# Attention probabilities with keys on the partitions, after a separate pass for the maxima, in a two-layer hybrid decoder trunk

## What is computed

```
# fox, one head of width 64
s = (q @ k.T) * 64**-0.5
s = s + cum[:, None] - cum_k[None, :]        # cumulated log forget gates
s = where(key <= query, s, -1e30)
out = softmax(s) @ v
# dsa, one head: the same without cum, and only over each query's topk = 64 keys
score = sum_j relu(iq_j @ ik.T / 8) * iw_j   # 16 indexer heads choose the keys
```

## Time and profile before

| | |
|---|---|
| median of 3 runs | 2811.59 us |
| the profiled execution | 2811.41 us, of which the span of the trace is 2809.6 us |
| busy share of the span | PE 95%, PE's weight loads 91%, DVE 63%, ACT 49%, POOL 0% |
| chain that ended last | PE 89%, DVE 6%, ACT 3%, issue 2%, DMA 1% |
| TensorE clock granted, mean over the span | 0.938 of full |
| layer 0, first indexer score to first product of the output projection | 333.26 to 504.68 us |

### The profile page before, as it was taken

How to read it: one execution, slowest core, us unless ns; L and a number is a source line. 1 busy time by engine, 2 the same in 40 slices (tenths; PEclk the granted TensorE clock), 3 DMA queues, 4 the chain that set the end, 5 groups by cost and what they waited for, 6 DMA issues and landing times.

```text
span 2809.6 us, 56056 instructions
## 1 busy us (share of the span) xinstructions
PE 2668.1 (95%) x21786; PEld 2548.4 (91%) x21786; DVE 1782.2 (63%) x2890; ACT 1366.1 (49%) x2051; POOL 11.9 (0%) x19
## 2 busy tenths in 40 slices
PE   5989999989999999999979899999899999999997
PEld 5989866989999999999979898669899999999997
DVE  6777555576666666544487775655766666665445
ACT  5444443456555555433364444444566665653333
POOL 0000000000000000000000000000000000000000
PEclk8999975899999999999999999659999999999999
DMA  4433210435555555554444332104355555555553
GB/s 170 146 113 127 76 45 1 150 120 179 179 173 177 172 173 171 180 173 166 165 146 150 107 127 77 38 1 163 115 194 182 182 180 179 184 184 186 173 183 112
DMA packets 109728, 401.84 MB, mean 143 GB/s; under 512 B 12176, under 2 KB 12176, under 8 KB 109584
## 3 DMA queue, kind: packets, MB, share of 16 engines
q1 hardware_dynamic: 108432, 395.15, 41.9%
q0 software_dynamic: 1152, 4.63, 0.4%
HBM read 397.50 MB, written 2.23 MB: 142 GB/s over the span
## 4 chain that ended last, share of the span: by engine, by line
PE 89%; DVE 6%; ACT 3%; issue 2%; DMA 1%; SPq 0%; ACTq 0%; DVEq 0%
PE ps L383 25%; PE ps L384 25%; PE ps L385 25%; PE ps L587 2%; PE ps L554 2%; PE ps L530 1%; PE ps L456 1%; PE ps L522 1%; PE ps L575 1%; PE ps L543 1%; PE ps L465 1%; DVE h L1047 1%; DVE h L1067 1%; ACT h L715 1%; PE ps L531 1%
## 5 line engine op out<-in xcount | busy, mean ns | idle before, releaser
L699 ACT ACTIVATE w_hi<-raw 128x1024 fp32r<-128x1024 f32 x728 | 763.6, 1057 | 935.3 <-PE ps L385 918.0
L384 PE MATMUL ps<-x_lo,w_hi 128*128 128x272 f32 (+1 forms) x3904 | 1122.1, 287 | 0.0
L385 PE MATMUL ps<-x_hi,w_hi 128*128 128x272 f32 (+1 forms) x3904 | 1120.2, 287 | 0.0
L992 DVE TENSOR_TENSOR w_lo<-raw,w_hi 128x1024 fp32r<-128x1024 f32 x592 | 716.8, 1224 | 616.3 <-ACT w_hi L699 616.2
L383 PE MATMUL ps<-x_hi,w_lo 128*128 128x272 f32 (+1 forms) x2816 | 805.5, 286 | 19.9 <-DVE x_lo L1075 19.3
L384 PEld LDWEIGHTS ps<-x_lo,w_hi 128*128 128x128 f32 x3904 | 741.3, 190 | 1.8
L385 PEld LDWEIGHTS ps<-x_hi,w_hi 128*128 128x128 f32 x3904 | 741.1, 190 | 0.0
L383 PEld LDWEIGHTS ps<-x_hi,w_lo 128*128 128x128 f32 x2816 | 530.8, 189 | 21.8 <-issue 19.2
L383 PE MATMUL ps<-g_hi,w_lo 128*128 128x272 f32 (+1 forms) x1408 | 403.9, 287 | 4.8 <-DVE w_lo L992 2.7
L384 PE MATMUL ps<-g_lo,w_hi 128*128 128x272 f32 (+1 forms) x1408 | 403.2, 286 | 0.0
L385 PE MATMUL ps<-g_hi,w_hi 128*128 128x272 f32 (+1 forms) x1408 | 401.2, 285 | 0.0
(11 more groups left out here) (257 smaller groups left out, 2977.6 us busy)
## 6 DMA issues: line engine op xcount, KB each, us to landing
raw<-stream SPq DMA_DIRECT2D x744, 512.0 KB, 3.3
h<-x SPq DMA_DIRECT2D x4, 544.0 KB, 6.2
out<-h SPq DMA_DIRECT2D x4, 544.0 KB, 2.7
cst<-consts POOLq DMA_DIRECT2D x2, 724.0 KB, 6.4
wkv<-w_kv POOLq DMA_DIRECT2D x2, 512.0 KB, 7.8
b_st<-ssm_b POOLq DMA_DIRECT2D x2, 512.0 KB, 9.2
c_st<-ssm_c POOLq DMA_DIRECT2D x2, 512.0 KB, 11.4
par<-params SPq DMA_DIRECT2D x1, 562.0 KB, 12.0
```

The lines of the kernel that those rows point to most:

```text
L384: pe.matmul(acc, w_hi[:, slot, kk, cols], lo, start=False, stop=False)
L385: mm = pe.matmul(acc, w_hi[:, slot, kk, cols], hi, start=False, stop=k == tiles - 1)
L699: act.activation(w_hi[:, slot, :, :], raw[:, slot, :, :], ACT.Copy).then_inc(hi_made, 1)
L992: dve.tensor_tensor(w_low(phase, slot), raw[:, slot, :, :], w_hi[:, slot, :, :].bitcast(F32), ALU.subtract).then_inc(in_lo_made if phase = ...
```

## The change

The attention is rewritten with keys on the partitions, so that the exponentials are already laid out as `weighted_values` needs them. Since a maximum over keys can't then be taken along the free axis, it comes from a first pass.

- First pass: `scores` stays, without the matmul that adds the query's cumulated gate (L524 of before). DVE takes the 24 maxima of a kind into `peaks`. Nothing else reads these scores. For fox the pass runs right behind the 48 indexer scores, and the four gate groups now follow it in one piece; for dsa it runs between the two kinds.
- `peak_transposes` turns the maxima into rows (3 transposes a kind), and ACT writes them negated into rows 64 to 71 or 96 to 103 of `cum`, which the selector `sel` now also picks. A second pass, `turned_scores`, computes the scores again for each head in three pieces of keys (272, 176 and 80 queries wide: only queries from the piece's own start on), subtracts the maximum by a matmul with `cum`, and adds the mask by matmuls (one a piece for fox; 3, 2 and 1 for dsa).
- ACT takes the exponential of a piece (for fox with the key's cumulated gate as bias, from `decays`). There is no sum, no transposition of probabilities and no copy: `v_tok` has 65 columns a head, the last of ones, and the product with it gives the denominator beside the 64 outputs (`weighted_values`, stationary probabilities always 96 columns wide). DVE's `normalise` divides all three query pieces of a head at once.
- `top_scores` has four of its eight rounds on DVE beside the gate groups, the others between fox heads. The mask is then made beside fox head 4.
- Output norms of a kind stand behind all its heads. New waits: PE waits for `yt_made` of fox before the dsa heads, and for `peak_made` before the heads of each kind.
- Beside the indexer: 3 more small transposes and `decays` (3), one copy of ones into `v_tok`, one memset of `probs`.

```diff
-S_BANKS = (4, 5, 3)
+KT_COLS = [NT - s for s, n in QT]
+KT_PAD = NQ * MASK_T - NT
+KT_AT = [sum(KT_COLS[:c]) + c * KT_PAD for c in range(NQ)]
+M_BANKS = ((0, 1, 2), (4, 5, 6))
+M_ROW = (64, 96)
+VH = HEAD + 1
...
             def scores(l, n):
-                s = ps[0:qn, S_BANKS[n % 3], 0:ke]
+                s = ps[0:qn, M_BANKS[kind][n % 3], 0:ke]
                 if n >= 3:
-                    pe.wait_ge(prob_made, l * 48 + n - 2)
+                    pe.wait_ge(max_made, l * UNITS + n - 2)
...
-                    pe.matmul(s, cum[:, qs:ke], sel_r[:, hd:hd + 1].to_broadcast([P, ke]), start=False, stop=False)
...
-            def prob_transposes(l, n):
...
+            def turned_scores(l, kind, hd):
+                for c, (ks, kn) in enumerate(QT):
+                    piece = 2 * u + min(c, 1)
+                    at = KT_COLS[1] if c == 2 else 0
+                    s = ps[0:kn, 4 + piece % 3, at:at + KT_COLS[c]]
+                    if piece >= 3 and c < 2:
+                        pe.wait_ge(prob_made, 4 * HEADS * l + piece - 2)
+                    pe.matmul(s, keys[b, ks:ks + kn], queries[b, ks:NT], start=True, stop=False)
+                    pe.matmul(s, row.to_broadcast([P, kn]), cum[:, ks:NT], start=False, stop=False)
+                    if kind == 0:
+                        mm = pe.matmul(s[:, 0:kn], causal_r[0:kn, 0:kn], ident_r[0:kn, 0:kn], start=False, stop=True)
+                    else:
+                        for q in range(c, NQ):
+                            mm = pe.matmul(s[:, qs - ks:qs - ks + qn], dsa_bias[0:qn, q, ks:ks + kn], ident_r[0:qn, 0:qn], ...)
+                    if c != 1:
+                        mm.then_inc(turned, 1)
...
+                for q, (qs, qn) in enumerate(QT):          # weighted_values
+                    for c in range(q + 1):
+                        at = KT_AT[c] + qs - ks
+                        mm = pe.matmul(ps[0:MASK_T, 7, q * VH:(q + 1) * VH], probs[0:kn, hd % 2, at:at + MASK_T],
+                                       v_tok[0:kn, kind, c, hd, :], start=c == 0, stop=c == q)
...
+            def attend(l, kind):
+                pe.wait_ge(peak_made, 2 * l + kind + 1)
+                for hd in range(HEADS + 1):
+                    if hd < HEADS:
+                        turned_scores(l, kind, hd)
+                    if hd:
+                        weighted_values(l, kind, hd - 1)
...
+                for n in range(48):
+                    index_scores(l, n)
+                for n in range(HEADS * NQ):
+                    scores(l, n)
+                pe.wait_ge(gelu_made, l + 1)
+                pe.wait_ge(max_made, l * UNITS + HEADS * NQ)
                 for g in range(4):
                     gate_group(l, g)
                 pe.wait_ge(idx_relu, 48 * (l + 1))
+                peak_transposes(l, 0)
+                attend(l, 0)
+                pe.wait_ge(glu_summed, l + 1)
...
+                pe.wait_ge(bias_made, l + 1)
+                for n in range(HEADS * NQ, UNITS):
+                    scores(l, n)
+                for q in range(NQ):
+                    output_transposes(l, 0, q)
+                peak_transposes(l, 1)
+                pe.wait_ge(yt_made, 6 * l + 3)
+                attend(l, 1)
...
+                negate_peaks(0)                              # ACT
+                for hd in range(HEADS):
+                    exponentials(0, hd)
+                for q in range(NQ):
+                    output_squares(0, q)
+                output_deviations(0)
...
+                maxima(0)                                    # DVE
+                for g in range(4):
+                    top_scores(g)
+                    gate_apply(g)
...
+                for hd in range(HEADS):
+                    if 4 + hd < TOPK // 8:
+                        top_scores(4 + hd)
+                    if 4 + hd == TOPK // 8:
+                        sparse_bias()
+                    normalise(0, hd)
+                maxima(1)
```

More of the change, by code:

```diff
@@ L532, in scores @@
                 mm.then_inc(score_made, 1)
-            def prob_transposes(l, n):
[L535 to L555, removed]
-                mm.then_inc(o_made, 1)
+            def peak_transposes(l, kind):
+                pe.wait_ge(max_made, l * UNITS + (kind + 1) * HEADS * NQ)
+                if kind:
+                    pe.wait_ge(o_read, 2 * HEADS * l + HEADS)
+                for q, (qs, qn) in enumerate(QT):
+                    mm = pe.transpose(ps[0:HEADS, 7, qs:qs + qn], peaks[0:qn, kind, q, :], const("ident", qn, qn))
+                mm.then_inc(peak_mm, 1)
@@ new lines, in _ @@
+                for j in range(2):
+                    mm = pe.matmul(ps[:, 0, 0:NT], ones[:, :], gate_sq[:, j, :], start=j == 0, stop=j == 1)
+                mm.then_inc(glu_ms, 1)
+                pe.wait_ge(bias_made, l + 1)
[6 more added lines that the diff above has]
+                attend(l, 1)
@@ L854, in _ @@
-                gate_out(4)
+                for n in range(48):
+                    qs, qn = QT[n % NQ]
+                    act.wait_ge(idx_mm, l * 48 + n + 1)
+                    if n >= 4:
+                        act.wait_ge(idx_used, l * 48 + n - 3)
+                    act.activation(relu[0:qn, n % 4, 0:qs + qn], ps[0:qn, 4 + n % 4, 0:qs + qn], ACT.Relu,
+                                   scale=SCALE).then_inc(idx_relu, 1)
+                for g in range(5):
+                    gate_out(g)
@@ L858, in output_squares @@
                     qn = QT[q][1]
[L859 removed]
+                    act.wait_ge(o_read, 2 * HEADS * l + (kind + 1) * HEADS)
                     if n:
@@ new lines, in _ @@
+                negate_peaks(0)
[4 more added lines that the diff above has]
+                output_deviations(0)
+                act.wait_ge(glu_ms, l + 1)
+                act.activation(rstd[:, :], ps[:, 0, 0:NT], ACT.Sqrt, bias=RMS_EPS, scale=1.0 / SSM_W).then_inc(glu_sd, 1)
+                negate_peaks(1)
+                for hd in range(HEADS):
+                    exponentials(1, hd)
+                    if hd in (1, 3):
+                        high_part((hd - 1) // 2)
+                    if hd == 5:
@@ L909, in _ @@
                         high_part(2)
-                    if n >= UNITS:
-                        output_squares(1, n - UNITS)
+                for q in range(NQ):
+                    output_squares(1, q)
                 output_deviations(1)
@@ new lines, in _ @@
+                maxima(1)
+                for q in range(NQ):
+                    output_scale(0, q)
+                for q in range(NQ):
+                    output_read(0, q)
+                dve.wait_ge(glu_sd, l + 1)
+                mark(dve.reciprocal(rstd[:, :], rstd[:, :]))
+                after()
+                for k in range(UT):
+                    last = dve.scalar_tensor_tensor(out=yssm[:, k, :], in0=yssm[:, k, :], scalar=param("mix_g", l * DT + k),
+                                                    in1=rstd[:, :], op0=ALU.mult, op1=ALU.mult)
+                    if k % 4 == 3:
+                        last.then_inc(ymul, 1)
@@ L1499, in _ @@
+                for hd in range(HEADS):
+                    normalise(1, hd)
+                    if hd in (2, 4, 6):
+                        low_y(hd // 2 - 1)
                 for q in range(NQ):
```

224 lines of the change are left out of this document (91 added, 133 removed).

## The result

The changed kernel takes **2911.73 us** (median of 4 runs, 2909.65 to 2913.6), the kernel before beside it 2813.23. The ratio is 1.0352, with a 95% interval from 1.0335 to 1.0369. The prediction was 2915 us. The span is 2907.7 us.

The account below looks back on a forecast made before the run. The prediction took PE's order of small products at the low clock, 1.2 GHz, as the bound. Terms summed to 223.3 us a layer against 171.4, 103.8 more over two layers: 2811.41 became 2915 us, range 2862 to 2948.

Parts of the forecast that it names:

- PE waits for nothing: Kernel before: DVE waits for PE's scores, PE for nothing; said against the rival that PE isn't the bound, chance 0.02.
- A triple: Three score units of the fox first pass at the low clock, without gate terms: 3.65 + 3 x 0.11 = 3.98 us.
- a fox head: Second pass, low clock: scores, changes back to 64 rows and twelve 96-column value records, 5.77 us; 46.2 us for eight.
- a dsa head: Second pass, low clock: as a fox head plus three more mask products at 0.16, 6.25 us; 50.0 us for eight.
- The indexer's 16.2: Indexer scores before the fox first pass: they hold PE for 16.2 us a layer, before and after the change.
- The gates' 30.4: Four gate groups at 7.60 us each, 30.4 us a layer, before and after the change.
- their slow start: Gates behind the fox first pass start at the low clock and lose 2.5 us, making 32.9 us.
- The gate term that goes: Gate product dropped from fox first-pass units: 0.23 us in the widest unit, 0.16 in the two others, at the low clock.
- The rival with one fast pass: Clock holds through fox's first pass, 18.9 instead of 29.7 us: 2888; with fox heads fast too, 2849; chance 0.15.
- Gaps: PE's waits before the heads: 2.9 us to the first fox head, 5.6 us to the first dsa head.
- DVE's division from PSUM: In each head, two DVE instructions divide three pieces at once: 0.4 to 1 us, under a head of 5.8 us.
- The rival that the clock stays up: Full clock everywhere in the attention: 154 us a layer, 17 less than before, 2777 us in all; chance 0.06.

Follow-up runs that it names:

- padded: The changed kernel with each head's queries copied by GpSimd into buffers whose other 64 rows are zero, products contracting both heads' keys: 2732.47 us.
- kernel with one idle product a head: The changed kernel plus never-read products of 128 rows by 272 columns: one a head, one per three first-pass units, others in PE's waits: 2876.92 us.
- kernel with full rows: The changed kernel with every key and query product contracting all 128 rows of its two-head tile, so scores differ from the reference's: 2739.56 us.
- padded kernel without passes: The changed kernel without first passes or maxima, with queries in zero-padded buffers and no constant-row product in the dsa heads: 2709.6 us.
- Three idle products a head: The changed kernel plus never-read products, three in each head and one per three first-pass units, others in waits: 2859.7 us.

## Why the prediction was right

The time lies 3 us from the forecast and inside the range of 2862 to 2948. The mechanism is the forecast one. That it came so close is partly luck: terms were off by up to 2 us in both directions, and 5 us came back outside the part that was priced.

- **What bounds.** PE at the low clock, before and after. Shown: in the first pass PE is busy 23.00 of 23.00 us at 0.50, and taking the passes out gives 124.8 us back. The remark that PE waits for nothing is too strong: between 381 and 405 us of the kernel before it waits 1.5 us in all for ACT and DVE, too little to change the sum.
- **Prices at the low clock.** A triple 3.98 us, found 4.04; a fox head 5.77, found 5.88; a dsa head 6.25, found 6.3. Every head term is a little low, 1.6 us for each kind of head, and the indexer and gates 1.3 and 2.0 high. The errors cancel: 223.3 against 222.4. The indexer's 16.2 held two waits of 0.51 us for relu, which are gone in the new order. The gates' 30.4 was 0.8 too high, since four groups in one piece take 29.60 us at full clock in the kernel without first passes, and their slow start cost 1.4 us where I had 2.5. The gate term that goes is that of L524, but I priced L525: the starts of L524 give 0.31, 0.27 and 0.19, 0.77 a head and not 0.55. The triple would then come to 3.76. That 3.98 was nearer to 4.04 is luck: the term that now follows the 64-row product (L528, 0.20, 0.27 and 0.31) takes the longer time that L524 took there.
- **Where the clock falls.** I let it fall 3 us into the fox first pass, and it fell after 5 to 6. The rival with one fast pass is out: the rest of that pass and all 16 heads of layer 0 were at 0.50, and so were those of layer 1 but for their first 0.7 us. The gates bring the clock back to 1.00, and it falls again at about 412.2 us, at the end of the wait of 2.57 us. That wait only brings the fall forward: in the kernel without first passes, which does not have it, the clock fell at 382.6 us, three microseconds into the first head and ahead of any wait in it.
- **Gaps.** 2.9 us ahead of the fox heads (found 2.9, of them 2.57 waiting for the negated maxima on ACT), 5.6 ahead of the dsa heads (found 5.1).
- **Costs at nothing.** The gates' new place: shown by the kernel that puts them back, 2913.49. DVE's division from PSUM did not pace the heads: PE is busy 46.84 of 47.60 us.
- **What was right for an incomplete reason.** I put the low clock down to the units and priced it, but not what in them causes it. The rival that the clock stays up was put at 2777 us; the change in that form (padded) takes 2732, because half rows also cost time at equal clock. By the page of the Trainium skill cited there (TensorE: Matmul & The Clock Gate, Part 4, on PE-mode transposes) the full clock does not engage in transpose mode, which would blame the transposes. The fox first pass has none among its units and ran at 0.50; the measurement decides.

## What to carry to other kernels

When a stretch of small products shows PE busy and the granted clock at half, look at the rows that they contract, and at how often the number changes, before counting them: a product on 64 rows can be padded with zeros to 128, here by an engine that was idle, and that gave 179 us of 2912. Then look at the waits: full rows did not always bring a fallen clock back. Price a rewrite at both clocks, since the order of two versions can turn: scores made twice cost 3.5% here, and with full rows the new version is the faster of the two. Idle products show what a clock is worth, and cost least in waits that exist anyway.

## What the runs showed of the hardware that was not expected

- The clock fell and stayed down without a wait: it fell at 425.7 us in the kernel with one idle product a head, and PE was busy 23.00 of 23.00 us at 0.50 in the changed kernel's first pass, with 64-row products; the same count of products and columns at 128 rows ran at 1.00 (fox first pass and fox heads of the padded kernel). Zeros in the added rows did as well as data.
- Full rows and a busy PE did not suffice either: behind the waits of the turn, dsa heads with 128 rows ran at 0.50 with PE busy 35.00 of 35.00 us (layer 1 of the kernel with full rows) and 34.00 of 34.00 us (layer 0 of the padded kernel without passes).
- A key tile with its 64-row product takes 0.96 us at full clock, with 128 rows 0.66, for the same columns. Why a change of rows costs time was not looked into. The indexer's products have 64 rows too and ran at 1.00 for their 15 us, so half rows are not enough by themselves; a kernel with 64 rows in every product was not tried.
- Three idle products a head held the clock, one did not (fall at 425.7 us). Where between them the limit lies, and what of rows, columns and waits the chip counts, stays open.
- The padded kernel without passes was slow for 54.6 us from the turn of layer 0 on and for 6.8 us at that of layer 1, with the same program. What ended each was not tested, only that filling the waits removes both. The same holds for the kernel with full rows, whose turn is slow for some six microseconds in layer 0 and for all heads in layer 1.
